# Hybrid pooling/S5/MoE block on one core: two experts combined on TensorE instead of one, last experts in loop order, projection of p moved

## The reference, cut to what matters

```python
# v = RMSNorm(h); top-1 of 4 groups, top-2 of its 8 experts -> combine[t, g, e]
for g in range(N_EXPERT_GROUPS):
    hg = silu(einsum('td,edf->tef', t, w_gate[g])) * einsum('td,edf->tef', t, w_up[g])
    hg = hg * combine[:, g, :, None]
    out = out + einsum('tef,efd->td', hg, w_down[g])
h = h + out
gate = sigmoid(rmsnorm(h, g_ple) @ ple_gate_w + ple_gate_b)
h = h + gate * (p @ ple_proj_w)
out = rmsnorm(h, g_final)
```

## Time and profile before

| | |
|---|---|
| median of 3 runs | 526.61 us (525.79 to 528.49) |
| the profiled execution | 527.02 us, span 525.3 us |
| PE busy | 476.9 us, 91% of the span |
| DVE, ACT, POOL busy | 238.8, 162.6, 159.8 us |
| DMA moved | 146.83 MB, mean 279 GB/s |
| mean granted TensorE clock | 0.984 |

### The profile page before, as it was taken

How to read it: one execution, slowest core, us unless ns; L and a number is a source line. 1 busy time by engine, 2 the same in 40 slices (tenths; PEclk the granted TensorE clock), 3 DMA queues, 4 the chain that set the end, 5 groups by cost and what they waited for, 6 DMA issues and landing times.

```text
span 525.3 us, 7242 instructions
## 1 busy us (share of the span) xinstructions
PE 476.9 (91%) x2723; PEld 269.1 (51%) x2723; DVE 238.8 (45%) x676; ACT 162.6 (31%) x262; POOL 159.8 (30%) x144
## 2 busy tenths in 40 slices
PE   0999999999999998989999999778999997599993
PEld 0655776634854477645555555444454453244441
DVE  2799998999233358622222222112111111564534
ACT  5634434456442344111111111021212112114464
POOL 1059999954100111212322222211212011003360
PEclk9999999999999999989999999899999999799998
DMA  8784300499289956999999999999999996960012
GB/s 296 138 194 90 72 0 1 151 136 209 106 362 424 412 241 260 398 417 388 421 419 415 418 412 416 420 418 420 421 418 421 418 405 241 360 281 1 0 80 80
DMA packets 57195, 146.83 MB, mean 279 GB/s; under 512 B 27722, under 2 KB 32870, under 8 KB 44360
## 3 DMA queue, kind: packets, MB, share of 16 engines
q1 hardware_dynamic: 50856, 133.92, 68.8%
q0 software_dynamic: 5904, 12.41, 6.1%
q10 hardware_dynamic: 400, 0.04, 0.1%
HBM read 138.17 MB, written 16.29 MB: 294 GB/s over the span
## 4 chain that ended last, share of the span: by engine, by line
PE 70%; DMA 22%; DVE 3%; ACT 2%; issue 1%; SPq 0%; ACTq 0%; POOLq 0%; DVEq 0%; POOL 0%
PE bank L1564 63%; DMA ring<-in_exp_w_up_dram 12%; DMA h<-in_exp_w_up_dram 6%; DMA moe<-v_d,gidx_all 2%; PE bank L1903 2%; PE bank L1649 1%; DMA ring<-in_ssm_a_im_dram 1%; DMA pairs_d<-moe,sidx_all 1%; PE bank L1587 1%; DMA big<-pairs_d 1%; PE bank L1922 1%; PE bank L2017 1%; ACT moe L529 1%; PE bank L1793 1%; DVE h L1320 1%
## 5 line engine op out<-in xcount | busy, mean ns | idle before, releaser
L1564 PE MATMUL bank<-ring,moe 128*64 128x256 f32 (+3 forms) x976 | 128.2, 388 | 3.3 <-DMA ring<-in_exp_w_up_dram 3.3
L1564 PEld LDWEIGHTS bank<-ring,moe 128*64 128x64 f32 (+1 forms) x976 | 76.6, 146 | 37.6 <-issue 14.0
L1491 POOL DMA_INDIRECT pairs_d<-moe,sidx_all x32 | 31.9, 998 | 167.3 <-ACT moe L529 119.8
L848 DVE TENSOR_TENSOR vrow<-moe,bank 64x128 f32<-64x128 f32 x64 | 18.6, 291 | 120.3 <-ACT moe L752 119.2
L1564 PE MATMUL bank<-ring,ut 128*128 128x512 f32 x128 | 57.2, 606 | 0.9 <-DVE ut L848 0.9
L1564 PE MATMUL bank<-big,ut 128*128 128x512 f32 x128 | 56.6, 595 | 1.1 <-ACT ut L674 1.1
L1564 PE MATMUL bank<-ut,big 128*128 128x512 f32 x128 | 57.3, 596 | 0.2 <-ACT ut L541 0.2
L752 ACT ACTIVATE moe<-bank 64x256 f32<-64x256 f32 x32 | 12.1, 377 | 141.2 <-PE bank L1564 141.2
L529 ACT ACTIVATE moe<-bank 128x512 f32<-128x512 f32 x56 | 32.5, 598 | 64.7 <-PE bank L1564 54.2
L1564 PE MATMUL bank<-big,moe 128*64 128x256 f32 (+1 forms) x264 | 43.5, 435 | 3.9 <-DMA zbuf<-in_exp_w_up_dram 3.1
L848 DVE TENSOR_TENSOR ring<-ring,bank 128x64 f32<-128x64 f32 (+1 forms) x142 | 39.5, 278 | 2.8
(11 more groups left out here) (185 smaller groups left out, 586.0 us busy)
## 6 DMA issues: line engine op xcount, KB each, us to landing
ring<-in_exp_w_up_dram SPq DMA_DIRECT2D x19, 1024.0 KB, 25.9
ring<-in_exp_w_down_dram SPq DMA_DIRECT2D x18, 1024.0 KB, 24.8
ring<-in_exp_w_gate_dram SPq DMA_DIRECT2D x17, 1024.0 KB, 20.4
big<-in_exp_w_gate_dram SPq DMA_DIRECT2D x7, 1024.0 KB, 18.0
big<-in_exp_w_down_dram SPq DMA_DIRECT2D x7, 1024.0 KB, 29.7
big<-in_exp_w_up_dram SPq DMA_DIRECT2D x6, 1024.0 KB, 18.3
big<-in_w_in_dram SPq DMA_DIRECT2D x2, 2048.0 KB, 11.9
ut<-in_exp_w_gate_dram SPq DMA_DIRECT2D x4, 1024.0 KB, 21.2
```

The lines of the kernel that those rows point to most:

```text
L848: return dve.tensor_tensor(o, a, b, op)
L1491: pool.indirect_dma_start(pairs, bass.IndirectOffsetOnAxis(ap=index, axis=0), at(moe, ALL, M_Y + k * 512, [[1, 512]]), None, bounds_check= ...
L1564: return pe.matmul(o, a, b, start=start, stop=stop, skip_group_check=loose)
```

## The change

Expert 30 is treated as expert 31 was: its slots get zero rows early, a matrix X30 is built and transposed, and `combined` multiplies both, adding in PSUM. Both matrices now carry the token's weight, so VectorE's last step of `combine` is a plain addition. Expert 30's scatter is gone. The order at the end is that of the loop (gate-up(31), then down(30)). `proj` stands before `down_step` and `pp_out` before `y_out`. The first half of a gate matmul group waits for the first half of `turned_g_ple` only. The loads of the gate weights are as before: the first half was in two parts already.

```diff
-            seq(pick(qv("rk31", [[1, NT]]), at(bank[5], ALL, NE - 1, [[NE, NT]]), 1.0,
-                     qv("MS", [[NE, NT]], NE - 1), ALU.add, ALU.mult))
-            pick(qv("X31", [[P, NT], [1, P]]), cv(C_PLACE, [[0, NT], [1, P]]), 1.0,
-                 qv("rk31", [[1, NT], [0, P]]), ALU.add, ALU.is_equal).then_inc(x1_done, 1)
+            for x in (NE - 2, NE - 1):
+                own.do(pick(qv(f"rk{x}", [[1, NT]]), at(bank[5], ALL, x, [[NE, NT]]), 1.0,
+                            qv("MS", [[NE, NT]], x), ALU.add, ALU.mult))
...
-                for k, col in ((1, S_W1), (2, S_W2)):
-                    own.do(tt(qv("wb", one, (k - 1) * NT), qv(f"M{k}", [[NE, NT]], NE - 1), at(small, ALL, col, one), ALU.mult))
-                own.settle()
-                own.do(tt(at(small, ALL, S_WT, one), qv("wb", one), qv("wb", one, NT), ALU.add))
+                for i, x in enumerate((NE - 2, NE - 1)):
+                    for k, col in ((1, S_W1), (2, S_W2)):
+                        own.do(tt(qv("wb", one, (k - 1) * NT), qv(f"M{k}", [[NE, NT]], x), at(small, ALL, col, one), ALU.mult))
+                    own.settle()
+                    own.do(tt(qv("wt", one, i * NT), qv("wb", one), qv("wb", one, NT), ALU.add))
+                    seq(pick(qv(f"X{x}", [[P, NT], [1, P]]), cv(C_PLACE, [[0, NT], [1, P]]), 1.0,
+                             qv(f"rk{x}", [[1, NT], [0, P]]), ALU.add, ALU.is_equal))
+                    tt(qv(f"X{x}", [[P, NT], [1, P]]), qv(f"X{x}", [[P, NT], [1, P]]), qv("wt", [[1, NT], [0, P]], i * NT),
+                       ALU.mult).then_inc(x1_done, 1)
...
+            def slots_30_out():
+
+                act.wait_ge(ppt_ps, 2)
+                copy(at(small, ALL, S_S30, [[1, 2 * P]]), bank[6][:, 0:2 * P], ppt_sb)
+                copy(at(rw, ALL, 0, [[1, 2 * P]]), bank[6][:, 2 * P:4 * P], ppt_sb)
...
-                if e + 2 < NE:
-                    silu(e + 1)
-                if e == 0:
-                    act.wait_ge(slot_done, 1)
-                y_out(e)
-                if e == NE - 2:
+                if e + 1 < NE:
                     silu(e + 1)
                 if e == P_ROWS:
                     p_rows_out()
                 if e in P_PROJ:
                     for n in range(2):
                         pp_out(2 * P_PROJ.index(e) + n)
+                if e == 0:
+                    act.wait_ge(slot_done, 1)
+                y_out(e)
+                if e == 0:
+                    slots_30_out()
...
-            rows_out(2, sidx_all[:, NE - 1:NE], ys_stored[2])
-            for e in range(NE - 1):
+            for x in (NE - 2, NE - 1):
+                rows_out(2, sidx_all[:, x:x + 1], ys_stored[2])
+            for e in range(NE - 2):
...
-                        dve.wait_ge(comb, 6 * t + 3 * n + k + 1)
+                        if k == 0:
+                            dve.wait_ge(comb, 6 * t + 2 * n + 1)
+                for n in range(2):
+                    hv = at(h, ALL, t * DM + n * 512, [[1, 512]])
                     dve.wait_ge(cmb_ps, 2 * t + n + 1)
-                    dve.scalar_tensor_tensor(hv, bank[2 * t + n][:, :], at(small, ALL, S_WT + t, [[1, 1]]), hv, ALU.mult, ALU.add
-                                             ).then_inc(comb, 1)
+                    dve.wait_ge(comb, 6 * t + 4)
+                    tt(hv, bank[2 * t + n][:, :], hv, ALU.add).then_inc(comb, 1)
...
-                    mm(bank[2 * t + n][:, :], at(ring, parts, E_S + t * P, [[1, P]]),
-                       at(moe, parts, M_Y + (NE - 1) % YBUF * 512, [[1, 512]]), True, True).then_inc(cmb_ps, 1)
+                    for x in (NE - 2, NE - 1):
+                        turned = (at(ring, parts, E_S + t * P, [[1, P]]) if x == NE - 1 else
+                                  at(small, parts, S_S30 + t * P, [[1, P]]) if t < 2 else at(rw, parts, (t - 2) * P, [[1, P]]))
+                        got = mm(bank[2 * t + n][:, :], turned, at(moe, parts, M_Y + x % YBUF * 512, [[1, 512]]),
+                                 x == NE - 2, x == NE - 1, True)
+                    got.then_inc(cmb_ps, 1)
...
-            slots_31()
+            slots(NE - 1)
+            slots(NE - 2)
+            pe.wait_ge(ppt_sb, 2)
             x_step(1)
...
-                if e == NE - 2:
-                    down_step(e)
                 if e + 1 < NE:
                     gu_step(e + 1)
-                if e != NE - 2:
-                    down_step(e)
                 if e == P_ROWS:
                     p_rows()
                 if e in P_PROJ:
                     for n in range(2):
                         proj(e, 2 * P_PROJ.index(e) + n)
+                down_step(e)
...
                 for j in range(KC):
+                    if j % 4 == 0:
+                        pe.wait_ge(ut_done, KC + 2 * NT + 2 * t + 1 + j // 4)
...
-                    pe.wait_ge(comb, 6 * t + 3 * n + 3)
+                    pe.wait_ge(comb, 6 * t + n + 5)
...
-                pe.wait_ge(ut_done, KC + 2 * NT + 2 * (t + 1))
                 gate(2 * t)
```

More of the change, by code:

```diff
@@ L178, in build @@
         S_A2, S_T1, S_T2 = 64, 64 + 4 * G, 64 + 6 * G
-        S_WT = S_A2
+        S_S30 = S_A2
         R_CW, R_CWN = 0, 4608
@@ L207, in build @@
         Z_SSM, Z_POOL = 0, NB * T
-        Q = {"oh": M_XG, "X1": M_XT + DM, "X31": M_XT + DM + NT * P}
+        Q = {"oh": M_XG, "X1": M_XT + DM, "X30": M_XT + DM, "X31": M_XT + DM + NT * P}
         q = 2 * DM
@@ L214, in build @@
                         ("q3", NT * 8), ("q4", NT), ("oh2", NT * 8), ("df", NT), ("ex", NT), ("dn", NT),
-                        ("M1", NT * 32), ("M2", NT * 32), ("MS", NT * 32), ("rk", 2 * NT), ("rk31", NT),
+                        ("M1", NT * 32), ("M2", NT * 32), ("MS", NT * 32), ("rk", 2 * NT), ("rk30", NT), ("rk31", NT), ("wt", 2 * NT),
                         ("rh", 2 * NT * 32), ("pm", 2 * NT),
@@ L328, in stores @@
         def stores(e):
-            return 16 * (e // YBUF + (e % YBUF == 2))
+            return 16 * (e // YBUF + 2 * (e % YBUF == 2))
         x_d = A["x"].rearrange("b s d -> (b s) d")
@@ L758, in y_out @@
                 copy(at(moe, ALL, M_Y + e % YBUF * 512, [[1, 512]]), bank[4 + e % 2][:, :], dn_sb)
+            def slots_30_out():
+                act.wait_ge(ppt_ps, 2)
+                copy(at(small, ALL, S_S30, [[1, 2 * P]]), bank[6][:, 0:2 * P], ppt_sb)
+                copy(at(rw, ALL, 0, [[1, 2 * P]]), bank[6][:, 2 * P:4 * P], ppt_sb)
             def p_rows_out():
-                act.wait_ge(ppt_ps, 2)
+                act.wait_ge(ppt_ps, 3)
                 for j in range(2):
@@ L1517, in _ @@
             for k in range(YBUF):
-                pool.wait_ge(ys_stored[k], 16 * len(range(k, NE - 1, YBUF)) + 16 * (k == 2))
+                pool.wait_ge(ys_stored[k], 16 * len(range(k, NE - 2, YBUF)) + 32 * (k == 2))
             def note(k):
@@ L1878, in proj @@
                 t, half = n // 2, n % 2
-                pe.wait_ge(ppt_sb, 2)
+                pe.wait_ge(ppt_sb, 4)
                 pe.wait_ge(xT_sb, e + 3)
@@ L1884, in proj, with slots @@
                 got.then_inc(pp_ps, 1)
-            def slots_31():
-                pe.wait_ge(x1_done, 3)
+            def slots(x):
+                pe.wait_ge(x1_done, 4 if x == NE - 1 else 3)
                 for t in range(NT):
-                    got = pe.transpose(bank[7][:, t * P:(t + 1) * P], at(moe, ALL, Q["X31"] + t * P, [[1, P]]), ident)
+                    got = pe.transpose(bank[7 if x == NE - 1 else 6][:, t * P:(t + 1) * P], at(moe, ALL, Q[f"X{x}"] + t * P, [[1, P]]), ident)
                 got.then_inc(ppt_ps, 1)
@@ L2000, in _ @@
                 pass
-            pe.wait_ge(ppt_sb, 3)
+            pe.wait_ge(ppt_sb, 5)
             pe.wait_ge(dn_sb, NE)
```

## The result

The changed kernel takes 525.47 us (median of 20 runs, 522.91 to 526.95); the kernel before, run beside it, takes 527.99 us (20 runs, 525.59 to 530.12). The ratio is 0.9946 [0.9931, 0.9962], about 2.85 us less (the two medians alone differ by 2.52). The profiled execution took 522.91 us with a span of 521.0, the fastest of its twenty, so its absolute times run ahead of the median.

- **a**, the first of the three loads that SyncE issues after down(0); **b**, its restart with the next three after down(1);
- **L**, the landing of the up weights of expert 31; **g**, the first gate matmul behind the loop.

What follows compares the result with a forecast made beforehand. The prediction took the weight loads and gaps in their queue to bound the expert loop. Its terms, +1.4 - 0.6 - 1.3 - 1.75 = -2.25 us, gave 524.8 against the profiled 527.02, hence a median of 524.4; range 522.4 to 527.4.

Steps and rivals of the forecast that it cites:

- Start of the loop: Added VectorE work delays `slot_done`, x_step(1) and the weights behind SyncE's restart: +1.4 us, bounds +0.4 and +2.5.
- Proj before down: In the expert loop, proj ahead of the down step gains nothing, since weights are late anyway: 0 us.
- Loop order: At the loop's end, gate-up(31) before down(30) gains nothing, since late up weights set gate-up(31)'s start: 0 us.
- The pairs: After the loop, pairs 0 is issued 2.9 us earlier, but the slowest DMA engine holds its landing: -0.6 us.
- rival C: Pairs 0 gains its whole 2.9 us and the first transposes wait for `combined`: -3.65 us, 522.9 us, chance 0.12.
- Combined hidden: Before the first transposes, 32 `combined` matmuls take 7.1 us instead of 3.70 for 16, hidden with 1.5 us cover.
- rival D: Doubled `combined` runs at half clock and becomes the bound: +3.1 us, 529.7 us, chance 0.06.
- Combine to first gate: From VectorE's combine(0) start to the first gate matmul, 5.3 us instead of 6.6: 1.3 us gained.
- The clock at the end: TensorE idles 1.5 us instead of 4.1, so the first gate group takes 6.87 instead of 8.62: 1.75 us gained.
- Rival A: The clock falls again at the end: +0.3 us in all, 526.9 us, chance 0.19.

Runs made afterwards that it cites:

- before_filled: The kernel before with the 16 `combined` matmuls of expert 31 issued twice, nothing else changed; ratio 0.9978 [0.9955, 1.0001].
- proj_only: The kernel before with only proj moved before the down step and pp_out before y_out; ratio 0.9980 [0.9958, 1.0002].
- pairs_late: The changed kernel with SyncE waiting for down(31) instead of down(30) before loading pairs 0; ratio 0.9987 [0.9959, 1.0016].
- pairs_first: `best` with the first part of the gate weights issued behind pairs 0 instead of ahead; ratio 0.9902 against the kernel before, median 522.39 us.
- old_order: The changed kernel with down(30) back before gate-up(31) on TensorE; ratio 0.9926 against the kernel before, median 523.08 us.
- best: The changed kernel with down(30) before gate-up(31) and two extra matmuls at the loop's start; ratio 0.9926 against the kernel before, median 523.49 us.

## Why the prediction was right, by its steps

The forecast was 524.4 us, the range 522.4 to 527.4, and "the same" the likeliest of the three at 0.54; measured is 525.47, 0.54% faster, just over the edge of 0.5%, with an interval that excludes a ratio of 1. The time lies in the range, but luck has a part in that. The forecast started from a median of 526.61 us of three runs, and the kernel before measured 527.99 beside the changed one, so the time came out 1.1 us above the forecast though the change gained more than was forecast. The mechanisms at the start and at the pairs held; the loop order's did not, the reason given for the largest term stays unproven, and the sizes of four terms were off in both directions and partly cancelled.

- **Start of the loop: +1.4, measured +0.6.** The passing on was right, one to one. `slot_done` moved by 3.0 us (3.2 were forecast). But x_step(1) came 1.0 us later, not 1.5: the two copies of X30 start 0.26 us apart, so ScalarE's three copies took from 225.30 to 226.45, 1.15 us instead of the 1.4 that were reckoned. Nor is 1.03 us after a the usual start of x_step(1) before: there it waits for a gather to land, and in the four variants it starts 1.33 to 1.58 us after a, so the change delays it by 0.4 to 1.0. The restart after a: without a fall of the clock 9.73 (`before_filled`) and 9.83 (`proj_only`) before, 10.39 after; with one 11.04, 11.37 and 11.58 before, 11.84 to 12.02 after. That is about 0.6 us either way, between the means. A fall costs 1.2 to 1.9 us more, and it comes in one trace and not in another of kernels that are alike up to there. It is not the only source of spread, nor shown to be the larger one: a itself lies between 224.4 and 228.9 us in the thirteen traces, and the two latest, `proj_only` and `pairs_late`, have another fall of the clock near 192.5 us, ahead of the loop.
- **Proj before down: 0.** Not refuted, not settled (`proj_only`).
- **Loop order: 0, measured a loss of 0.4 to 0.8.** The weights did set the start of gate-up(31), as said. The step failed in what the wait does: with down(30) moved behind, TensorE idled 2.36 to 2.59 us in one stretch, the clock fell to 0.50 between 0.6 us before and 0.5 us after the end of it, and the block took 6.75 to 7.08 us in each of the five kernels with this order. g - L is 18.83 to 19.17 in the three of them that change nothing behind this step, against 18.42 and 18.37 with the old order.
- **The pairs: -0.6, measured -1.4** (14.27 to 12.89 us after L), past the bound of 1.1. That the transfer ahead of pairs 0 holds back its landing was the right mechanism: an issue 2.5 us earlier against L (6.9 us after it, before 9.4) moved the landing by 1.4, rival C's 2.9 us did not come (the prediction's own numbers, 436.73 + 5.9 + 1.1 = 443.7, give 2.6 and not 2.9), and `pairs_first` shows the order in the queue to be what counts. Mis-sized was the missing scatter. The gate's first part, ahead of pairs 0, landed 0.7 us sooner against L, where I had allowed 0.4: 11.1 or 10.9 us after L in the five kernels with expert 30's scatter, 10.3 to 10.4 in the seven that lack it and keep the order of issue. No run takes away the scatter alone, so that it is the cause is argued, not shown. And the distance behind it shrank from 3.2 to 2.5 us, what the prediction's division gave for 1 MB and I did not take in full; that is the earlier issue, as the other traces under `pairs_late` show. One late engine fits the share of 0.06 just before the landing; but that is only the last microsecond. In the kernel before the share goes down from 1.06 in the microsecond from 437 over 0.60 from 441 to 0.22 from 443, so several engines seem to end one after another, and which engine holds the landing was not seen. The Trainium skill (DMA: Bandwidth & Descriptors, "Latency and other measured facts") has two of the 16 engines usually slower than the others: the trace agrees in so far as the engines end at different times. The 525.0 us that I had worked out by it, with no gain from the pairs at all, lies nearer to the measured 525.47 than the forecast, but by luck: pairs 0 did gain 1.4 us.
- **Combined hidden: wrong by 0.5 to 0.9 us.** Its 32 matmuls ran at full clock (7.21 us), so rival D is out. But as gate-up(31) lasted longer and pairs 0 came sooner, the cover of 1.5 us was used up: VectorE had the first half of h at about 452.9, the transposes began at 453.56. From VectorE's start to the transposes it is 4.38 us in the changed kernel and 4.55 to 4.75 in three others with its order, against 3.84 in `old_order`, where the block before runs at full clock and the cover is there.
- **Combine to first gate: -1.3.** From VectorE's start to the gate 6.60 before; 5.91 in the changed kernel, for the reason just given, so this term measured -0.7. It is 5.37 in `old_order` and `best`, against a forecast of 5.3.
- **The clock at the end: -1.75, measured -1.5** (8.62 to 7.11; I had taken half of a 13.73 us group). The fall before came at 454.1 us, by the share of 0.56 in the earlier trace rows, and not after 454.5 as the prediction reads it. This term was the largest, and it came as forecast, but the reason given is not borne out: the prediction went by the one stretch of idle time ahead of the first transposes (1.5 us instead of 4.1), and `before_filled` had 0.74 us there and lost the clock. It left out the waits behind that stretch (1.57 and 0.88 us there). Whether their sum or the pieces decide stays open, so this term was right in part by luck.

The measured terms: +0.6 at the start, 18.83 - 20.90 = -2.07 from L to the gate, -1.5 for the first group: -2.97 (with the 19.17 of other traces -2.6), against about -2.85 by the ratio. The forecast's -2.25 was short by what the pairs and the start gave, less what the loop order and the doubled `combined` took. Rival A did not come in any of the eight kernels with expert 30 combined. Open is how often the clock falls at the start in either kernel: a trace shows one execution.

## What to carry to other kernels

When a queue runs full to its end, find its last restart: here each microsecond there reached the last weights unchanged. At its end a transfer issued early enough (3 us ahead, here) landed a fixed time behind the one issued before it, so reordering the issues helped where hurrying one no longer did. A wait that "costs nothing" because data are late anyway cost 0.4 to 0.8 us here, as TensorE idled in one stretch ahead of a dense block; put movable matmuls into it, as the old order did with down(30). When asking what keeps the clock, list every idle stretch up to the dense block, not the longest alone. Compare traces by distances between events, and repeat where one kernel's runs spread over 4 us and the effects are half a microsecond.

## What the runs showed of the hardware

- The clock at the end was lost and kept behind the same matmuls: 32 `combined` matmuls with three short idle stretches behind them (0.74, 1.57, 0.88 us) lost it, the same 32 with 2.57 and 0.21 us kept it. Whether the pieces or the sum (3.19 against 2.78 us) decides was not found.
- At the end of the queue one transfer of 1 MB landed 2.5 to 2.6 us behind the one before it, in six kernels, issued 3.1 to 4.8 us ahead of that landing; issued 2.5 us ahead, 2.8 us behind; 1.7 to 1.9 us ahead, 3.1 to 3.7 us behind; 0.76 us ahead, 4.8 us behind.
- ScalarE's copies of 128x256 out of PSUM show 0.38 us each, but two in a row start 0.26 us apart (225.80 and 226.06 us in the changed kernel).
